# Experts' weights in transfers of 2 MB: pairs of places of a ring

## What is computed

```python
D_MODEL, SEQ = 1024, 256
N_EXPERTS, TOP_K, EXPERT_FF = 8, 2, 3584

def swiglu(h, w1, w3, w2):
    return (jax.nn.silu(h @ w1) * (h @ w3)) @ w2

def moe_swiglu(h, w_router, w1, w3, w2):
    ...
    logits = (t @ w_router).astype(jnp.float32)
    top_vals, top_idx = lax.top_k(logits, TOP_K)
    gates = jax.nn.softmax(top_vals, axis=-1)
    combine = jnp.sum(jax.nn.one_hot(top_idx, N_EXPERTS, dtype=jnp.float32) * gates[..., None], axis=1)
    y = jnp.zeros_like(t)
    for e in range(N_EXPERTS):
        y = y + combine[:, e:e + 1].astype(t.dtype) * swiglu(t, w1[e], w3[e], w2[e])
    return y.reshape(B, S, D)
```

## Time and profile before

| | |
|---|---|
| median of 3 runs | 1408.83 us (1408.64 to 1410.14) |
| the profiled execution | 1406.07 us |
| its span (first to last instruction) | 1404.2 us |
| granted clock of TensorE, mean | 0.998 |
| busy: TensorE, VectorE, ScalarE | 1384.3, 1129.6, 951.4 us |
| read from HBM | 430.95 MB |
| loads of experts' weights | 336, 1024 KB each |

### The profile page before, as it was taken

The page is one execution under the profiler, slowest core; times in us unless marked ns, Lnnn a source line. Parts: engine busy times, 40 slices in busy tenths (PEclk is TensorE's granted clock), DMA queues, the critical chain, the costliest instruction groups (busy, mean ns, idle before and its releaser), DMA issues.

```text
span 1404.2 us, 19670 instructions
## 1 busy us (share of the span) xinstructions
PE 1384.3 (99%) x7055; PEld 1177.5 (84%) x7055; DVE 1129.6 (80%) x998; ACT 951.4 (68%) x908; POOL 108.8 (8%) x150
## 2 busy tenths in 40 slices
PE   7999999999999999999999999999999999999998
PEld 7788999988888888888888888888888888888886
DVE  5785655566776988998898888899888889888987
ACT  5765433345665877876877777786688777778773
POOL 4421000000102200000000000000000000000012
PEclk9999999999999999999999999999999999999999
DMA  9526655545524999999999999999999999999994
GB/s 326 189 72 216 230 189 179 181 155 204 212 87 157 354 403 369 371 389 386 344 385 389 349 400 381 380 353 384 392 342 393 382 368 383 384 384 354 383 378 177
DMA packets 155729, 433.77 MB, mean 309 GB/s; under 512 B 13780, under 2 KB 43649, under 8 KB 155690
## 3 DMA queue, kind: packets, MB, share of 16 engines
q1 hardware_dynamic: 147584, 422.49, 80.8%
q0 software_dynamic: 4656, 7.08, 1.4%
q10 hardware_dynamic: 3450, 3.69, 0.9%
HBM read 430.95 MB, written 13.38 MB: 316 GB/s over the span
## 4 chain that ended last, share of the span: by engine, by line
PE 96%; DVE 1%; ACT 1%; issue 1%; DMA 1%; POOL 0%; SPq 0%; DVEq 0%; POOLq 0%; ACTq 0%
PE ps L1623 88%; PE ps L1618 4%; PE ps L1762 2%; PE ps L1784 1%; DMA raw<-in_a_w_dq 1%; DVE wl_a L1082 0%; ACT wh_a L717 0%; DVE kT L1229 0%; PE ps L1630 0%; PE ps L1846 0%; ACT hth L738 0%; DVE htl L1111 0%; DVE bias L1244 0%; ACT h2h L934 0%; PE ps L1995 0%
## 5 line engine op out<-in xcount | busy, mean ns | idle before, releaser
L1082 DVE TENSOR_TENSOR wl_a<-raw,wh_a 128x2048 fp32r<-128x2048 f32 (+1 forms) x229 | 512.2, 2269 | 101.4 <-ACT wh_a L717 101.3
L717 ACT ACTIVATE wh_a<-raw 128x2048 fp32r<-128x2048 f32 (+1 forms) x230 | 433.7, 1909 | 154.1 <-PE ps L1623 142.6
L1082 DVE TENSOR_TENSOR wl_b<-raw,wh_b 128x2048 fp32r<-128x2048 f32 x168 | 378.1, 2285 | 15.9 <-ACT wh_b L717 15.8
L717 ACT ACTIVATE wh_b<-raw 128x2048 fp32r<-128x2048 f32 x168 | 317.8, 1925 | 54.5 <-PE ps L1623 32.1
L1623 PE MATMUL ps<-wh_a,hth 128*128 128x512 f32 (+2 forms) x576 | 223.6, 388 | 2.0 <-DVE htl L1111 1.6
L1623 PE MATMUL ps<-wh_a,htl 128*128 128x512 f32 (+2 forms) x576 | 222.1, 386 | 0.0
L1623 PE MATMUL ps<-wl_a,hth 128*128 128x512 f32 (+2 forms) x576 | 221.7, 385 | 0.0
L1623 PE MATMUL ps<-wh_b,hth 128*128 128x512 f32 x448 | 175.9, 393 | 0.3 <-DVE htl L1427 0.3
L1623 PE MATMUL ps<-wh_b,htl 128*128 128x512 f32 x448 | 174.4, 389 | 0.0
L1623 PE MATMUL ps<-wl_b,hth 128*128 128x512 f32 x448 | 174.3, 389 | 0.0
L1623 PEld LDWEIGHTS ps<-wh_a,hth 128*128 128x128 f32 x576 | 108.2, 188 | 23.9 <-DVE wl_a L1082 2.5
(11 more groups left out here) (269 smaller groups left out, 2003.8 us busy)
## 6 DMA issues: line engine op xcount, KB each, us to landing
raw<-in_moe_w SPq DMA_DIRECT2D x336, 1024.0 KB, 8.1
raw<-in_ffn_w SPq DMA_DIRECT2D x33, 1024.0 KB, 5.3
raw<-in_a_w_o SPq DMA_DIRECT2D x4, 1024.0 KB, 9.3
raw<-in_b_w_q SPq DMA_DIRECT2D x4, 1024.0 KB, 5.0
raw<-in_kv_w_k SPq DMA_DIRECT2D x4, 1024.0 KB, 5.1
raw<-in_kv_w_v SPq DMA_DIRECT2D x4, 1024.0 KB, 5.5
raw<-in_b_w_o SPq DMA_DIRECT2D x4, 1024.0 KB, 5.2
bias<-bias_wide ACTq DMA_DIRECT2D x8, 384.0 KB, 3.3
```

Source lines behind the costliest of these rows:

```text
L717: nc.scalar.activation(dst[:, 0:w], raw[:, n % RAW, 0:w], ACT.Copy).then_inc(hi_done, 1)
L1082: nc.vector.tensor_tensor(l[:, 0:w], raw[:, n % RAW, 0:w], h[:, 0:w].bitcast(fp32), ALU.subtract).then_inc(lo_done, 1)
```

## The change

Two neighbouring units of an expert are loaded by one transfer of 2 MB. It starts when both places of the ring are free, and it counts the semaphore of the first place alone; ScalarE waits for that one, for either unit. The other weights are loaded as before. The two loads of `y_rows` stay two transfers, both behind one wait for both places, and count a new semaphore `y_here`, on which VectorE waits once for both.

```diff
+            def load_pair(n, src, shape, j=0, j_units=0):
+
+                a, b = shape
+                dst = raw[:, n % RAW:n % RAW + 2, :].rearrange("p s (a b) -> p (s a) b", b=b)
+                sp.wait_ge(lo_done, n - RAW + 2 + j * j_units)
+                sp.dma_start(dst, src).then_inc(raw_here[n % RAW], 16)
...
                 def up_units(c, v, k):
                     rows_ = 2048 // e_width(c)
-                    for h in range(e_units(c)):
-                        load(U_MOE + k + h, v[:, ds(e * DC + rows_ * h, rows_), c * EW:c * EW + e_width(c)],
-                             (rows_, e_width(c)), j, U_RUN)
+                    for h in range(0, e_units(c), 2):
+                        load_pair(U_MOE + k + h, v[:, ds(e * DC + rows_ * h, 2 * rows_), c * EW:c * EW + e_width(c)],
+                                  (rows_, e_width(c)), j, U_RUN)
 
                 def down_units(c):
                     k = e_first("down", c)
-                    for h in range(e_units(c)):
-                        load(U_MOE + k + h, m2_v[:, ds(e * (EFF // P) + c * (EW // P) + 2 * h, 2), :], (2, D), j, U_RUN)
+                    for h in range(0, e_units(c), 2):
+                        load_pair(U_MOE + k + h, m2_v[:, ds(e * (EFF // P) + c * (EW // P) + 2 * h, 4), :], (2, D), j, U_RUN)
...
             sp.wait_ge(y_put, runs * 16 + Y_INIT)
+            sp.wait_ge(lo_done, U_MOE - RAW + 2 + runs * U_RUN)
             for r in range(2):
-                load(U_MOE + r, y_rows[r * HALF_ROWS:r * HALF_ROWS + SEQ, :].rearrange("(t p) d -> p t d", p=P), (T, D), runs, U_RUN)
+                sp.dma_start(raw[:, U_MOE % RAW + r, :].rearrange("p (t d) -> p t d", t=T),
+                             y_rows[r * HALF_ROWS:r * HALF_ROWS + SEQ, :].rearrange("(t p) d -> p t d", p=P)).then_inc(y_here, 16)
...
-                act.wait_ge(raw_here[n % RAW], 16 * (n // RAW + 1) + j * (16 * j_units // RAW))
+                first = n - n % 2 if moe_unit >= 0 else n
+                act.wait_ge(raw_here[first % RAW], 16 * (n // RAW + 1) + j * (16 * j_units // RAW))
...
             def add_rows():
 
+                dve.wait_ge(y_here, 16 * 2)
                 for r in range(2):
                     n = U_MOE + r
-                    dve.wait_ge(raw_here[n % RAW], 16 * (n // RAW + 1) + runs * (16 * U_RUN // RAW))
```

More of the change, by code:

```diff
@@ L278, in trunk_kernel @@
         raw_here = [sem(f"raw_here{i}") for i in range(RAW)]
+        y_here = sem("y_here")
         hi_done = sem("hi_done")
```

## The result

The changed kernel took 1417.37 us (median of 7 runs, 1411.31 to 1421.15), the kernel before 1408.64 us beside it (7 runs, 1405.67 to 1410.14). The ratio is 1.0058, with a 95% interval of 1.0046 to 1.0071: slower by 0.58%, about 8 us. The forecast of no change was wrong. What happened is the rival that had 0.06, and its price, not its mechanism, was the part that came out smaller: 8 us where it says 18.

What follows compares the result with a forecast made beforehand. TensorE was taken to bound the kernel, with loads running ahead. The terms summed to a span of 1404.2 + 0 + 0 + 0 + 0 = 1404.2 us; forecast at the runs' median 1408.8 us, range 2.4 us below to 2.7 above.

Steps and rivals of the forecast that it cites:

- The forecast of no change: Whole kernel: the time stays at 1408.8 us, given a chance of 0.91.
- the rival that had 0.06: Experts' loads: the ring of three pairs feeds too slowly; at 5.75 us a pair 18 us lost, 1427; chance 0.06.
- The bound, and what the issues cost: Experts: TensorE sets the pace, loads run ahead; 168 fewer issues of 373 ns on SP's queue are worth 0.
- The time of a lone pair: Experts' loads, empty queue: a pair lands 2.35 + 5.14 = 7.5 us after the second's issue.
- the DMA engines need 5.14: Experts' loads: a pair takes 5.14 us of the DMA engines, against 5.64 us of TensorE.
- the 2.35 us of delay: Each expert load: the part of 4.9 us to landing that is not bandwidth, which other loads fill.
- the sentence against the rival that fell: Ring of pairs: 8.4 us of a round is not bandwidth, the other two pairs give 10.3 us of DMA work.
- The cover: Experts' thinnest place 3.1 us; high halves of units 6 and 7 shift 3.5 us, leaving unit 6 4.8 us; loss 0.
- The first expert and the end: First expert: unit 10's high half moves 2.3 us, 3.5 us of cover left; end: rows' loads have 6 us; loss 0.
- The signs: Profile after: 168 loads, median 8 to 11 us; ScalarE's load wait 80 to 180; expert period 118.3; 405 to 412 GB/s.

Runs made afterwards that it cites:

- e1: Kernel before, 1 MB loads kept, but an expert's two neighbouring units are issued together when both places are free: 1409.77 us, ratio 1.0005.
- e2: Kernel before, 1 MB loads issued as before, but ScalarE touches the first of a pair only when both have landed: 1408.74 us, ratio 0.9998.
- e8: Kernel before with five of its six ring places in use for the experts' loads, all else the same: 1408.06 us, ratio 1.0.
- e7: Changed kernel, VectorE leaves out the last quarter of each low half from an expert's unit 4 on, loads whole: 1409.48 us, ratio 1.0012 to kernel before.
- e5: No model: SP alone streams 48 MB of experts' weights ten times, varying transfer size and number under way; 1 MB with two 336 GB/s, with three 410.
- e9: Kernel before with four of its six ring places in use for the experts' loads, all else the same: 1457.39 us, ratio 1.0364.
- e4: Changed kernel, the last eighth of each row of the experts' loads left out, same issues and waits: 1407.56 us, ratio 1.0001 to kernel before.

## Why the prediction was wrong, step by step

**The bound, and what the issues cost: right.** TensorE bounded the kernel before; e1, e2 and e8 each take away some cover and cost nothing. 168 fewer issues gave nothing back.

**The time of a lone pair: right.** I had 7.5 us. SP's line of the pair loads after the change, first all 168, then single loads: units 6 and 7, the pair that I followed, in the second expert and in the third, and one of a later expert:

```profile
DMA to landing us min/median/max: 7.5/10.1/12.3
...
L447 SPq DMA_DIRECT2D raw<-in_moe_w x1: 373/373/373, 571.4 to 571.4; - x1
DMA to landing us min/median/max: 9.2/9.2/9.2
...
L447 SPq DMA_DIRECT2D raw<-in_moe_w x1: 373/373/373, 690.4 to 690.4; - x1
DMA to landing us min/median/max: 7.6/7.6/7.6
...
L447 SPq DMA_DIRECT2D raw<-in_moe_w x1: 373/373/373, 975.2 to 975.2; - x1
...
DMA to landing us min/median/max: 11.1/11.1/11.1
```

**The step that failed: "the DMA engines need 5.14", with the 2.35 us of delay as something "that other loads fill".** ScalarE in time after the change (start us, us, what, idle before), where it waited for a pair:

```profile
472.74 1.92 ACT L728 ACTIVATE wh_a<-raw 128x2048 fp32r<-128x2048 f32 x1 [3.55 <-DMA raw<-in_moe_w]
...
574.00 1.28 ACT L728 ACT_TABLE_LOAD   x1 [2.54 <-DMA raw<-in_moe_w]
...
580.75 3.73 ACT L728 ACTIVATE wh_b<-raw 128x2048 fp32r<-128x2048 f32 x2 [0.76 <-DMA raw<-in_moe_w]
...
978.70 1.92 ACT L728 ACTIVATE wh_b<-raw 128x2048 fp32r<-128x2048 f32 x1 [1.58 <-DMA raw<-in_moe_w]
...
986.38 3.72 ACT L728 ACTIVATE wh_a<-raw 128x2048 fp32r<-128x2048 f32 x2 [3.96 <-DMA raw<-in_moe_w]
...
992.27 3.72 ACT L728 ACTIVATE wh_b<-raw 128x2048 fp32r<-128x2048 f32 x2 [2.17 <-DMA raw<-in_moe_w]
```

ScalarE takes each pair as it lands, so these starts are landings to 0.1 us. The pair issued at 571.4 had 2.5 us of lead (the one ahead landed at 573.9) and landed 6.7 us after it. The one issued at 975.2 had 3.4 us of lead, more than the 2.35 us of delay, and still landed 7.7 us after the one ahead, not 5.14. The next, which was issued over 5 us ahead, needed 5.9. Single pairs scatter (the one issued at 582.5 had 3.4 us of lead too and came 5.0 us behind), but the means are plain. Over all pairs of this trace, the 36 pairs issued 5 us or more before the one ahead lands come 5.1 us behind it; the 60 with 4 to 5 us of lead 5.5 us, the 57 with 3 to 4 us 6.2 us. So in this kernel a pair wants near 5 us of lead, not 2.35.

What makes up the difference is not shown. My reading is the 16 DMA engines: for one pair their completions in the trace come within 2.4 us of each other (median; 1.7 for a 1 MB load before), an engine that is done early needs the next pair then and not when the last is done, and 2.35 + 2.4 = 4.7 us is near the lead that is wanted. The Trainium skill, page "DMA: Bandwidth & Descriptors", section "Why a DMA increments its semaphore by 16 and not by 1", says that a transfer's engines finish independently and that only the full 16 increments mean that all data has landed; the trace agrees, with that spread.

For the reading speaks the trace of e7: its 35 pairs with 3.5 to 5 us of lead, whose predecessors had a spread of only 0.6 us, came 5.2 us behind them, and the 94 such pairs after the change (spread 2.3) 5.7. Against it: among the 122 pairs after the change with 2.5 to 5 us of lead, the lateness doesn't grow with the spread of the pair ahead (correlation -0.19). Nor does the spread belong to the size: in e5 it is 0.5 us for 2 MB with two under way, and 1.7 for 1 MB with two. It may be what sets the wanted lead, or another mark of a stream that has lost its lead.

**And the ring can't give that lead.** This is the sentence against the rival that fell: "8.4 us, while the other two pairs give the DMA engines 10.3 us of work; the stream then stops only when the ring is full and ahead". If pairs come s us apart, a round of the ring is 3s. From a pair's landing until its places are issued again takes 6.7 us (the chain: 1026.67 to 1033.38; 7.06 on average over the 8 rounds, since VectorE has other work in some). From issue to landing there is then 3s - 7.06, and of lead 2s - 7.06. At the DMA engines' own 5.14 that is 3.2 us, which the stream doesn't bear; at TensorE's 5.63 it is 4.2, still too short; at the measured 5.77 it is 4.5, among the leads at which pairs came 5.5 to 6.2 us apart. In the terms of my sum, the part of a round that is not bandwidth was 8.4 us: 2.35, and 3.7 + 2.3 = 6.0 from landing to reissue. Measured are near 5 and 7.06, together 12.1 us, more than the 10.3 us of the other two pairs and more even than the 11.3 that TensorE takes for them.

With single places the lead at full rate is the other places' steps less one unit's handling (912.75 to 917.28 in the chain of e9, 4.5 us): 5 x 2.57 - 4.5 = 8.3 us for six places, 5.8 for five, 3.2 for four. A 1 MB load would by the same reading want 2.35 + 1.7 = 4.1, and the cliff stands between five and four. That four lose as much as 3.6% it doesn't give: at TensorE's pace four places have 3 x 2.82 - 4.5 = 4.0 us of lead, and by that should lose next to nothing. VectorE's other work inside the round is my guess for the rest.

In e4 a full pair takes 4.5 us and may come 1.1 later; in e7 the handling is a microsecond shorter. e1 keeps the single landings, and e2 the single issues, which fits that each alone is free. So the runs show that the loss goes away with shorter loads or with an earlier issue; why a pair wants near 5 us of lead stays open, since no run changed the spread alone.

**The cover: the right place, read once.** At the thinnest place VectorE began the low halves of units 1 and 2 at 797.26 + 5.54 before. VectorE in time after, in the second and third experts:

```profile
569.12 4.48 DVE L1093 TENSOR_TENSOR wl_b<-raw,wh_b 128x2048 fp32r<-128x2048 f32 x2
...
582.70 4.49 DVE L1093 TENSOR_TENSOR wl_b<-raw,wh_b 128x2048 fp32r<-128x2048 f32 x2 [0.39 <-ACT wh_b L728]
...
688.06 4.48 DVE L1093 TENSOR_TENSOR wl_b<-raw,wh_b 128x2048 fp32r<-128x2048 f32 x2
```

The second expert begins at 563.58: again + 5.54, exactly the 3.1 us of cover. The third begins at 681.88: + 6.18, 0.6 us less. The low halves of units 6 and 7 begin in the second at + 19.1, where I had 814.6 - 797.26 = 17.3. The first is done 2.28 us later, at + 21.4, and TensorE begins unit 6 at + 24.5 as before: cover 3.1 us, not 4.8. ScalarE's high halves begin at + 17.2, where I had + 15.4. So the shift at this place was 5.2 us for my 3.5, because the pair ahead was still under way. One place with cover left was taken for all, but the loss is a rate: a little with every pair, 0.14 us in the bound stretch (5.77 - 5.63), which the units split ahead hide for more than two experts.

**The first expert and the end: right.** Unit 10's high half begins at 472.74, 19.6 us after the expert's first matmul, and 19.6 was forecast (469.7 - 450.15). No wait for the experts' rows stands at the end.

**The price of the rival: right in its rate, wrong in its reach.** At "5.75 us a pair", a value that it took by way of example, the rival had 2.3 us an expert, 18 in all. The measured rate in the bound stretch is 5.77 us, and the loss 2 to 3 us an expert, but only from the third expert on: 12.0 us in this execution, 8 in the median.

**The signs.** 168 loads of 2048 KB, median 10.1, minimum 7.5 us: right, and so was that ScalarE's wait for TensorE falls (`wh_a`: 116.3 us for 142.6). ScalarE's waits for the loads (215 for 80 to 180) and the full stretch (391 GB/s for 405 to 412) were wrong. And the chain shows what was named as the sign of a wrong prediction: periods over 118.6 us, with low halves (`wl_b`) and loads in it.

## What to carry to other kernels

For a ring that feeds a bound engine, write down the round: places x pace, less the time from landing to reissue, less one transfer. What is left is the lead, and it has to exceed more than the delay of a lone load: here near 5 us for 2 MB, where the delay is 2.35. That the bandwidth suffices says nothing. How much lead a stream wants is read from a trace, by setting each load's lead against its landing. Merging transfers halves the places, and where three or more 1 MB loads are under way the streams of e5 show nothing that it could give. And look for small losses per step over the whole run, since one expert with cover left, or two, can be living on stock.

## What of the hardware was not expected

- One 1 MB load at a time moves 203 GB/s, two 336, three 410; two of 2 MB also 410. The Trainium skill, page "DMA: Bandwidth & Descriptors", section "Bandwidth", gives 341 GB/s for 1 MB and 425 for 16 MB, measured on another path of issue (GpSimd), and the rule to batch to 1 MiB or more. The 336 with two under way is near its 341. With two under way a larger size still helps here (388 at 1.5 MB, 410 at 2 MB), but so does a third 1 MB load, and from there on a larger size adds nothing.
- A delay of 2.35 us between issue and full flow needs more than 2.35 us of lead to be hidden: 1.5 MB with two under way, at a lead of 4.1 us, still ran at 388 GB/s.
- The lead that 2 MB wants isn't one number: the pairs of e7 kept 5.2 us apart at 3.5 to 5 us of lead, those of the changed kernel did not (5.7 us).
- Two waits that cost nothing that can be told apart cost 0.3% together.
